# A planner that counts the transfers as one queue, and the loads of a half head as three items

## The chip, the cores and the metric

One core of a Trainium2 chip runs the whole program. The metric is the device time of one execution in microseconds; three runs of the kernel before took 1387.27 to 1389.36, median 1388.89.

## What is computed

One residual block over 1024 tokens of 1024 features, in float32. Cut to what matters here:

```python
h = rms_norm(x, pre_mix_norm)
fq, fk, fv, ff, gq, gk, gv, gb, ga, gz = split(h @ w_in)
# A: 8 heads of 64, causal attention with a bias of gate sums
logits = q @ k.T * scale + cum[q] - cum[k]          # masked
fox_o = rms_norm(softmax(logits) @ v)
# B: 4 heads of 128, delta rule by chunks, then a scan over the chunks
m = strict(k_beta @ k.T * decay);  t_inv = inverse(eye + m)
u = t_inv @ v_beta;  w = t_inv @ (k_beta * exp(gc))
v_new = u - w @ state;  o = q_dec @ state + a_intra @ v_new
state = state * g_last + k_dec.T @ v_new
gdn_o = rms_norm(o) * silu(gz)
x = x + rms_norm(concat(fox_o, gdn_o) @ w_out)
x = x + rms_norm(square(relu(rms_norm(x) @ w_up)) @ w_down)
```

## The kernel before

The program has four stages: the input projection (to about 312 us; its results go to DRAM and come back head by head), the heads' stage (to about 639 us), the output projection, and the two products of the feed-forward part. The change touches the heads' stage alone.

Work of the heads' stage is cut into items. For each of four heads p of kind B there are *fills* (a PSUM bank filled by four transposes or by four or eight products of 128 x 128, then read by one other engine): turned inputs (fv, k, q, v, z), the turned keys knT, the products N (the matrix to be inverted) and A, then X, TX and XR, which build the inverse level by level, and at last W and U. The smallest blocks of the inverse, 16 x 16, are made on DVE: SP's item *gather* brings the diagonal blocks of n_low to DRAM and into 64 lanes (lane_n), DVE's four *lane* items invert them, and SP's *scatter* brings lane_t by way of t_dram into t_low. X and XR at the first level need t_low. I call the time from the last N product to the first X product a lane phase; there are four. The chunks' *scan* (scan_v, scan_o on PE, v_new and state on DVE, o on ACT) follows for each head. Beside that run 64 *tiles* of attention of kind A, eight for each of the eight half heads n: queries (high part on ACT, low part q_lo on POOL), scores (PE), max (DVE, the row minimum), exp (ACT), turn and copy (PE, then ACT or DVE), pv (PE), out (ACT). A half head needs its keys kk_raw (split by ACT and DVE into k_hi and k_lo), its queries q2 (two buffers) and its gate sums cum_row (two buffers). The item *fox* of SP, load_fox, issued all three: kk and q2 as two transfers of 256 KB each, cum as one of 512 KB. Every other load of a head (c_raw_k, q, v, z, v_fox, the decay row) has 512 KB, w_out_raw too. The ends of heads are *tails*: a mean on DVE, a power on POOL, and norms on DVE.

The order is made when the program is built. plan (line 514 on) simulates five queues (PE, ACT, DVE, POOL, SP) with a cost for each item, takes at each step the item that can start first, and breaks ties by the longest way to the end, which is times FOX_SHARE for attention items. follows (and pe_follows to sp_follows) tells what an item waits for. For SP, sp_cost (line 280) gave each item a time held and a time to landing, whatever else was under way. Each engine then runs its items strictly in the order ORDER, so a wait of one item holds all behind it on its engine. On PE, fills take turns in three banks.

At the end of the stage POOL makes eight low parts of w_out (big_lo, w_lo_part), and the first mixed tile is turned on PE (turn_mixed) when the norm that norms_of(0) counts is done, in the order of DVE's norms.

Of the kernel before, what the change touches and what calls it, by code (L numbers as in the profile page):

```python
# [18 lines left out]
NT = SEQ // P  # L19
# [191 lines left out]
for _c in range(KT):  # L211
# [11 lines left out]
    "sp": [(("load", "fv", 0), 0.0), (("load", "k", 0), 0.0), (("load", "v", 0), 0.4), (("load", "fox", 0), 1.7), (("load", "q", 0), 2.9),  # L223
           (("load", "g", 0), 5.2), (("load", "z", 0), 19.9), (("stored",), 22.7), (("load", "fox", 1), 28.2)],
# [55 lines left out]
def sp_cost(item):  # L280

    if item[0] in ("gather", "scatter"):
        return (5.6, 7.0) if item[0] == "gather" else (6.0, 6.9)
    return (3.2, 6.5) if item[:2] == ("load", "fox") else (0.45, 4.5)


def times_of(engine, item):

    if engine == "sp":
        return sp_cost(item)  # L290
    cost = {"pe": pe_cost, "act": act_cost, "dve": dve_cost, "pool": pool_cost}[engine](item)
    return cost - OVERLAP[engine], cost + PASSED_ON[engine]
# [64 lines left out]
def act_follows(kind, n=None, c=0):  # L357
# [14 lines left out]
    if kind == "exp":  # L372
        return [("dve", "max", n)] + [("dve", "tail_mean", ("fox", n // NT - 2, n % NT // HT))] * (n >= 2 * NT and n % HT == 0)
# [22 lines left out]
def dve_follows(kind, n, c=0):  # L396
# [42 lines left out]
def pool_follows(kind, n):  # L439
# [9 lines left out]
    if kind == "z":  # L449
        return [reader((n, "z", 1, 0))]  # L450
# [3 lines left out]
def sp_follows(kind, what, n=0):  # L454
# [8 lines left out]
    if what == "fox":  # L463
        return [("dve", "k_lo", n - 1), ("pool", "queries", NT * (n - 1) - 1), ("dve", "max", NT * (n - 1) - 1)]
# [47 lines left out]
def plan():  # L512
# [7 lines left out]
    free, fills, open_keys = dict(FREE_FROM), [item[1] for item in order["pe"] if item[0] == "fill"], set(keys)  # L520
# [12 lines left out]
    while open_keys:  # L533
# [8 lines left out]
        held, passed = times_of(key[0], key[1:])  # L542
        free[key[0]], done[key] = start + held, start + passed
# [10 lines left out]
FOX_SHARE = 1.0  # L554
# [128 lines left out]
def build(nc, x, pre_mix_norm, w_in, fox_f_bias, fox_out_norm, gdn_conv_w, gdn_a_log,  # L683
# [7 lines left out]
    with ExitStack() as ctx:  # L691
# [593 lines left out]
        def _(sp):  # L1285
# [188 lines left out]
            for item in ORDER["sp"][len(BEGUN["sp"]):]:  # L1474
# [10 lines left out]
                if what == "fox":  # L1485
                    load_fox(n)
# [1553 lines left out]
        def _(pe):  # L3040
# [242 lines left out]
            def scan_second(h, c):  # L3283
# [238 lines left out]
```

## Time and profile before

| | |
|---|---|
| median of 3 runs | 1388.89 us (1387.27 to 1389.36) |
| the profiled execution, device time | 1389.17 us |
| its span | 1386.7 us |
| PE busy in the span | 1319.8 us, 95% |
| DVE, ACT, POOL busy | 918.7, 645.6, 540.9 us |
| mean granted clock of PE | 0.979 |
| DMA, mean over the span | 129 GB/s |

All durations below are of the one profiled execution. Its times count from the start of the span; the device time is 2.5 us longer than the span. A granted clock of 1.00 is 2.4 GHz, one of 0.50 is 1.2 GHz; a value between is a mean over a stretch.

### The profile page before, as it was taken

What the parts mean: (1) busy time and instruction counts of PE and PEld (TensorE: products, weight loads), DVE (VectorE), ACT (ScalarE), POOL (GpSimd) and SP (SyncE); (2) the same over time, 40 slices, a digit from 0 to 9 for tenths busy, and PEclk for the clock granted to TensorE, in tenths of its full rate; (3) what the DMA queues carried; (4) which work ended last, traced back from release to release, by engine and by line L of the source; (5) the groups of instructions that cost most, each with busy time, mean ns of one, the idle gap of its engine ahead of it and who ended that gap; (6) DMA issues with size and microseconds to landing.
All of it is one profiled execution on the core that took longest, in us unless ns stands there. A gap on an engine that the chain in (4) does not pass through costs nothing.

```text
span 1386.7 us, 19443 instructions
## 1 busy us (share of the span) xinstructions
PE 1319.8 (95%) x6800; PEld 1111.0 (80%) x6800; DVE 918.7 (66%) x1506; ACT 645.6 (47%) x1381; POOL 540.9 (39%) x438
## 2 busy tenths in 40 slices
PE   5999999998899999998999899999999999999996
PEld 4778888887798989887887688888887888888885
DVE  6977776657678786753557996555555674444567
ACT  6655333446657576663335332333322444445453
POOL 3742333214423332334013776656563354441001
PEclk9999999999899999998999999999999999999999
DMA  6233223346514142043222455434535983334433
GB/s 198 62 123 121 78 85 112 122 152 204 162 33 123 46 119 57 9 107 92 82 85 77 122 188 167 149 125 143 167 137 192 374 283 99 99 94 159 157 93 150
DMA packets 145319, 178.58 MB, mean 129 GB/s; under 512 B 19852, under 2 KB 92860, under 8 KB 145224
## 3 DMA queue, kind: packets, MB, share of 16 engines
q1 hardware_dynamic: 145224, 177.35, 40.0%
q8 instruction: 55, 0.90, 0.3%
q14 instruction: 40, 0.33, 0.1%
HBM read 124.31 MB, written 53.00 MB: 128 GB/s over the span
## 4 chain that ended last, share of the span: by engine, by line
PE 78%; DVE 11%; DMA 3%; issue 3%; ACT 3%; POOL 1%; SPq 1%; DVEq 0%; ACTq 0%; POOLq 0%
PE ps L3425 7%; PE ps L3427 7%; PE ps L3426 7%; PE ps L3438 6%; PE ps L3439 6%; PE ps L3440 6%; PE ps L3082 6%; PE ps L3084 6%; PE ps L3083 6%; PE ps L3131 5%; PE ps L3266 3%; PE ps L3377 2%; PE ps L3379 2%; PE ps L3378 2%; PE ps L3252 2%
## 5 line engine op out<-in xcount | busy, mean ns | idle before, releaser
L3438 PE MATMUL ps<-db_hi,da_hi 128*128 128x512 f32 x448 | 175.3, 391 | 4.0 <-DVE db_lo L2718 4.0
L3439 PE MATMUL ps<-db_lo,da_hi 128*128 128x512 f32 x448 | 174.4, 389 | 0.0
L3440 PE MATMUL ps<-db_hi,da_lo 128*128 128x512 f32 x448 | 174.3, 389 | 0.0
L2716 DVE TENSOR_TENSOR da_lo<-a_raw,da_hi 128x512 fp32r<-128x512 f32 x112 | 85.6, 764 | 121.0 <-ACT da_hi L2124 120.9
L2124 ACT ACTIVATE da_hi<-a_raw 128x512 fp32r<-128x512 f32 x112 | 70.7, 631 | 159.1 <-PE ps L3440 138.1
L3425 PE MATMUL ps<-bt_hi,ring_hi 128*128 128x512 f32 x320 | 127.2, 397 | 5.1 <-DVE ring_lo L2638 5.1
L3427 PE MATMUL ps<-bt_hi,ring_lo 128*128 128x512 f32 x320 | 126.1, 394 | 0.0
L3426 PE MATMUL ps<-bt_lo,ring_hi 128*128 128x512 f32 x320 | 125.7, 393 | 0.0
L3082 PE MATMUL ps<-i_bt_hi,i_ring_hi 128*128 128x512 f32 x280 | 111.0, 396 | 3.0 <-DVE i_ring_lo L2216 1.6
L3084 PE MATMUL ps<-i_bt_hi,i_ring_lo 128*128 128x512 f32 x280 | 110.3, 394 | 0.0
L3083 PE MATMUL ps<-i_bt_lo,i_ring_hi 128*128 128x512 f32 x280 | 110.0, 393 | 0.0
L3438 PEld LDWEIGHTS ps<-db_hi,da_hi 128*128 128x128 f32 x448 | 84.1, 188 | 24.9 <-DVE db_lo L2718 7.7
L3440 PEld LDWEIGHTS ps<-db_hi,da_lo 128*128 128x128 f32 x448 | 84.1, 188 | 17.7
L3439 PEld LDWEIGHTS ps<-db_lo,da_hi 128*128 128x128 f32 x448 | 84.1, 188 | 17.0
L2948 POOL TENSOR_TENSOR o_rs<-o_ms,halves 128x1 f32<-128x1 f32 x24 | 16.5, 687 | 206.2 <-DVE o_ms L2616 94.7
L2023 ACT ACTIVATE ring_hi<-s_w 128x512 fp32r<-128x512 f32 x64 | 40.3, 632 | 120.6 <-PE ps L3427 118.9
L2718 DVE TENSOR_TENSOR db_lo<-wd,db_hi 128x512 fp32r<-128x512 f32 x112 | 88.7, 792 | 0.0
L2895 POOL TENSOR_TENSOR q_lo<-q,q_hi 128x128 fp32r<-128x128 f32 x64 | 31.1, 486 | 129.9 <-ACT q_hi L1860 127.3
L3266 PE MATMUL ps<-v_tok,probs_t 128*128 128x64 f32 x576 | 80.4, 278 | 1.4 <-ACT probs_t L1849 1.2
L3266 PEld LDWEIGHTS ps<-v_tok,probs_t 128*128 128x128 f32 x576 | 76.6, 202 | 2.8 <-ACT probs_t L1849 2.0
L3425 PEld LDWEIGHTS ps<-bt_hi,ring_hi 128*128 128x128 f32 x320 | 60.8, 190 | 18.5 <-DVE ring_lo L2638 5.6
L3427 PEld LDWEIGHTS ps<-bt_hi,ring_lo 128*128 128x128 f32 x320 | 60.6, 189 | 14.3
(382 smaller groups left out, 3447.7 us busy)
## 6 DMA issues: line engine op xcount, KB each, us to landing
a_raw<-act_dram SPq DMA_DIRECT2D x112, 256.0 KB, 2.6
act_dram<-s_act SPq DMA_DIRECT2D x64, 256.0 KB, 2.2
wd<-in_w_down_dram SPq DMA_DIRECT2D x15, 1024.0 KB, 7.7
act_dram<-c SPq DMA_DIRECT2D x48, 256.0 KB, 4.8
w_top<-in_w_up_dram SPq DMA_DIRECT2D x18, 512.0 KB, 4.2
w_bot<-in_w_up_dram SPq DMA_DIRECT2D x16, 512.0 KB, 5.4
i_top<-in_w_in_dram SPq DMA_DIRECT2D x14, 512.0 KB, 3.9
i_bot<-in_w_in_dram SPq DMA_DIRECT2D x14, 512.0 KB, 5.2
```

The lines of the kernel that those rows point to most:

```text
L2716: nc.vector.tensor_tensor(da_lo[s][:, :], a_raw[n % 4][:, :], da_hi[s][:, :].bitcast(F32), ALU.subtract).then_inc(d_lo_ready, 1)
L2718: nc.vector.tensor_tensor(db_lo[s][:, :], d_moving(n), db_hi[s][:, :].bitcast(F32), ALU.subtract).then_inc(d_lo_ready, 1)
L3082: nc.tensor.matmul(acc, i_ring_hi[r][:, k, :], b_hi[:, k, :], start=(first and k == 0), stop=False, skip_group_check=True)
L3083: nc.tensor.matmul(acc, i_ring_hi[r][:, k, :], b_lo[:, k, :], start=False, stop=False, skip_group_check=True)
L3084: last = nc.tensor.matmul(acc, i_ring_lo[r][:, k, :], b_hi[:, k, :], start=False, stop=(k == HK - 1), skip_group_check=True)
L3266: last = nc.tensor.matmul(fox_o(i)[:, 0:FOX_DIM], probs_t[n % 2][:, kb - 4 * c, :], v_tok[h % 2][:, kb, hh * FOX_DIM:(hh + 1) * FOX_DIM], ...
L3425: nc.tensor.matmul(acc, ring_hi[r][:, k, :], b_hi[:, k, :], start=(first and k == 0), stop=False, skip_group_check=True)
L3426: nc.tensor.matmul(acc, ring_hi[r][:, k, :], b_lo[:, k, :], start=False, stop=False, skip_group_check=True)
L3427: last = nc.tensor.matmul(acc, ring_lo[r][:, k, :], b_hi[:, k, :], start=False, stop=(k == HK - 1), skip_group_check=True)
L3438: nc.tensor.matmul(acc, da_hi[s][:, cols], db_hi[s][:, :], start=start, stop=False, skip_group_check=True)
L3439: nc.tensor.matmul(acc, da_hi[s][:, cols], db_lo[s][:, :], start=False, stop=False, skip_group_check=True)
L3440: return nc.tensor.matmul(acc, da_lo[s][:, cols], db_hi[s][:, :], start=False, stop=stop, skip_group_check=True)
```

## The change

The item ("load", "fox", n) becomes three, ("load", "kk", n), ("load", "q2", n) and ("load", "cum", n), each with its own condition. The planner keeps a time `wire` up to which the transfers are busy: a load lands no sooner than the queue of transfers ahead of it allows, and gather and scatter are made of hops and of eight pieces. Some conditions that the order of an engine must keep are added (exp after exp, o_square after o_square, z after z). FOX_SHARE goes from 1.0 to 0.9. A condition on the banks of the late scan in scan_second now names the first late item of the list. No instruction is added or removed; all five orders are new from the third item or so on.

```diff
-            to("sp", "load", "fox", n)
+            for what in ("kk", "q2", "cum"):
+                to("sp", "load", what, n)
...
-def sp_cost(item):
-
-    if item[0] in ("gather", "scatter"):
-        return (5.6, 7.0) if item[0] == "gather" else (6.0, 6.9)
-    return (3.2, 6.5) if item[:2] == ("load", "fox") else (0.45, 4.5)
+HOP, PIECES, PIECE_LANDS = 1.95, 3.8, 1.6
+
+
+def sp_times(item, start, wire):
+
+    if item[0] == "gather":
+        hop = max(start + PIECES, wire) + PIECE_LANDS
+        return hop + 0.5, hop + 0.1 + HOP, wire
+    if item[0] == "scatter":
+        hop = max(start, wire) + HOP
+        return hop + PIECES, hop + PIECES + PIECE_LANDS, wire
+    count = 2 if item[1] in ("kk", "q2") else 1
+    wire = max(start + 2.3, wire) + (2.2 if item[:2] == ("load", "g") else 1.12 * count)
+    return start + 0.5 * count, wire + 0.2, wire
...
     if kind == "exp":
-        return [("dve", "max", n)] + [("dve", "tail_mean", ("fox", n // NT - 2, n % NT // HT))] * (n >= 2 * NT and n % HT == 0)
+        return [("dve", "max", n)] + [("act", "exp", n - 1)] * (n >= 1) + [("dve", "tail_mean", ("fox", n // NT - 2, n % NT // HT))] * (n >= 2 * NT and n % HT == 0)
...
-    if what == "fox":
-        return [("dve", "k_lo", n - 1), ("pool", "queries", NT * (n - 1) - 1), ("dve", "max", NT * (n - 1) - 1)]
+    if what in ("kk", "q2", "cum"):
+        return [("dve", "k_lo", n - 1) if what == "kk" else ("pool", "queries", NT * (n - 1) - 1) if what == "q2" else ("dve", "max", NT * (n - 1) - 1)]
...
-        held, passed = times_of(key[0], key[1:])
-        free[key[0]], done[key] = start + held, start + passed
+        if key[0] == "sp":
+            free["sp"], done[key], wire = sp_times(key[1:], start, wire)
+        else:
+            held, passed = times_of(key[0], key[1:])
+            free[key[0]], done[key] = start + held, start + passed
...
-FOX_SHARE = 1.0
+FOX_SHARE = 0.9
...
-                if what == "fox":
-                    load_fox(n)
+                if what == "kk":
+                    load_kk(n)
+                elif what == "q2":
+                    load_q2(n)
+                elif what == "cum":
+                    load_cum(n)
...
-                if late and c == 0:
+                if (h, c) == LATE_SCANS[0]:
                     fills_read()
-                elif late:
+                if late and c > 0:
                     pe.wait_ge(o_read, n)
```

**SP in the first lane phase**, from the decay row of head 1, which follows the gather (n_dram, lane_n), to the scatter (t_dram, t_low). q_ is the buffer q2, v_fox the item fv. Before:

```order
L1364 DMA decay<-gate_dram 128x1024 [waits dve_prep]
L1359 DMA v_fox<-proj_dram 128x1024 [waits proj_stored1,filled]
L1353 DMA c_raw_z<-proj_dram 128x1024 [waits proj_stored1,filled]
L1407 DMA w_out_raw_135<-in_w_out_dram 128x8x128
L1374 DMA kk_raw<-proj_dram 64x1024 [waits proj_stored1,k_lo_ready]
L1374 DMA kk_raw<-proj_dram 64x1024
L1383 DMA q_0_145<-proj_dram 64x1024 [waits proj_stored1,q_ready]
L1383 DMA q_0_145<-proj_dram 64x1024
L1393 DMA cum_row_164<-gate_dram 128x1024 [waits fox_max]
L1353 DMA c_raw_z<-proj_dram 128x1024 [waits proj_stored1,filled]
L1462 DMA t_dram<-lane_t 64x256 [waits lane_step]
L1471 DMA t_low<-t_dram 16x8x16 [waits cleared,lanes_moved]
```

And now:

```order
L1380 DMA decay<-gate_dram 128x1024 [waits dve_prep]
L1369 DMA c_raw_q<-proj_dram 128x1024 [waits proj_stored0,pool_prep,filled]
L1399 DMA q_0_145<-proj_dram 64x1024 [waits proj_stored1,q_ready]
L1399 DMA q_0_145<-proj_dram 64x1024
L1375 DMA v_fox<-proj_dram 128x1024 [waits proj_stored1,filled]
L1390 DMA kk_raw<-proj_dram 64x1024 [waits proj_stored1,k_lo_ready]
L1390 DMA kk_raw<-proj_dram 64x1024
L1369 DMA c_raw_z<-proj_dram 128x1024 [waits proj_stored1,filled]
L1423 DMA w_out_raw_135<-in_w_out_dram 128x8x128
L1409 DMA cum_row_164<-gate_dram 128x1024 [waits fox_max]
L1478 DMA t_dram<-lane_t 64x256 [waits lane_step]
L1487 DMA t_low<-t_dram 16x8x16 [waits cleared,lanes_moved]
```

The queries c_raw_q of head 1 stood ahead of the gather and now come behind it; kk of half head 2 has gone ahead of the gather, and kk of half head 3 has come in; the z load of head 2 (the second c_raw_z of before) now follows the scatter. PE's fills of these queries, which stood 17.9 us of work into the stage's list, now stand at 22.7, those of z at 27.1 instead of 23.6.

**POOL at the start of the stage**, from the clearing of t_low. Before:

```order
L2921 MEMSET t_low 128x1024 [waits i_done,i_lo_ready]
L2895 TENSOR_TENSOR q_lo_172<-q_0_145,q_hi_170 128x128 [waits q_hi_ready]
L2864 TENSOR_TENSOR powers<-means,plus_half 128x4 [waits dve_prep] x2
L2879 TENSOR_TENSOR kd_147<-kn,gates_all 128x512 [waits filled,dve_prep]
L2869 TENSOR_TENSOR decay<-decay,const 128x1024 [waits act_prep]
```

And now:

```order
L2941 MEMSET t_low 128x1024 [waits i_done,i_lo_ready]
L2884 TENSOR_TENSOR powers<-means,plus_half 128x4 [waits dve_prep]
L2915 TENSOR_TENSOR q_lo_172<-q_0_145,q_hi_170 128x128 [waits q_hi_ready]
L2884 TENSOR_TENSOR powers<-means,plus_half 128x4 [waits dve_prep]
L2899 TENSOR_TENSOR kd_147<-kn,gates_all 128x512 [waits filled,dve_prep]
```

One power has gone ahead of the first low half of the queries.

**DVE at the end of the stage**, to the first low part of the turned mixed tiles (fox_rr and fox_ms are the mean of half head 7's second half, gdn_ms those of head 3, mixed_half the norms). Before:

```order
L2509 SCALAR_TENSOR_TENSOR fox_rr<-row_sum 128x4 [waits fox_read]
L2511 TENSOR_TENSOR fox_ms<-fox_ss,fox_rr 128x4 [waits rr_ready]
L2495 SCALAR_TENSOR_TENSOR state<-state,g_last_179,ps 128x128 [waits state_ready,scan_done]
L2505 TENSOR_TENSOR gdn_ms<-gdn_ss,q_eps 128x4 [waits gdn_square_done]
L2519 SCALAR_TENSOR_TENSOR mixed_half_160<-mixed_half_160,fox_ms,fox_norm_row 128x64 [waits masks_ready,tail_power] x4
L2527 SCALAR_TENSOR_TENSOR mixed_half_159<-mixed_half_159,gdn_ms,z_tok_158 128x128 [waits z_normed,tail_power] x4
L2527 SCALAR_TENSOR_TENSOR mixed_half_160<-mixed_half_160,gdn_ms,z_tok_158 128x128 [waits z_normed,tail_power] x4
```

And now:

```order
L2525 TENSOR_TENSOR gdn_ms<-gdn_ss,q_eps 128x4 [waits gdn_square_done]
L2529 SCALAR_TENSOR_TENSOR fox_rr<-row_sum 128x4 [waits fox_read]
L2531 TENSOR_TENSOR fox_ms<-fox_ss,fox_rr 128x4 [waits rr_ready]
L2547 SCALAR_TENSOR_TENSOR mixed_half_159<-mixed_half_159,gdn_ms,z_tok_158 128x128 [waits z_normed,tail_power] x4
L2547 SCALAR_TENSOR_TENSOR mixed_half_160<-mixed_half_160,gdn_ms,z_tok_158 128x128 [waits z_normed,tail_power] x4
L2539 SCALAR_TENSOR_TENSOR mixed_half_160<-mixed_half_160,fox_ms,fox_norm_row 128x64 [waits masks_ready,tail_power] x4
```

The norms of head 3 now stand ahead of those of half head 7's second half; POOL's last three powers have changed places in the same way, and among its eight big_lo parts POOL has one more low half of queries and one power.

## Rows read from the trace of the kernel before

**Rows 1.** Stretches: length, busy (x) of PE, PEld, DVE, ACT, POOL, PEclk, DMA share, GB/s.
```profile
350.00:380.00 30.00, 24.44 (x152) 21.90 (x150) 20.41 (x54) 19.07 (x61) 13.58 (x12) 0.77 0.59 165
380.00:420.00 40.00, 39.84 (x345) 38.19 (x345) 29.94 (x81) 22.28 (x74) 9.99 (x13) 1.00 0.16 43
420.00:445.00 25.00, 22.18 (x154) 20.29 (x152) 20.26 (x56) 17.73 (x60) 8.52 (x8) 0.86 0.55 156
...
490.00:510.00 20.00, 16.80 (x115) 14.65 (x115) 17.81 (x47) 16.28 (x57) 10.13 (x11) 0.91 0.32 90
...
570.00:593.00 23.00, 19.64 (x136) 18.11 (x136) 15.83 (x52) 12.07 (x43) 6.56 (x8) 0.85 0.07 12
...
632.00:650.00 18.00, 13.19 (x62) 11.32 (x62) 8.32 (x21) 3.83 (x11) 7.31 (x6) 0.72 0.40 118
```

**Rows 2.** Waits of PE, 320 to 640 us: us in total, times, longest.
```profile
PE ps L3234 <- DVE row_min L2477: 5.1, 7, 1.2
PE ps L3355 <- DVE mixed_half L2527: 4.0, 1, 4.0
```

**Rows 3.** Timeline, start of the stage: start us, us, engine, line, instruction [idle <-releaser].
```profile
323.96 0.83 POOL L2895 TENSOR_TENSOR q_lo<-q,q_hi 128x128 fp32r<-128x128 f32 x1
...
326.18 0.66 PE L3136 MATMUL ps<-const,kn 128*128 128x128 f32 x4 [0.83 <-DVE kbg L2375]
```

**Rows 4.** Chain of waits at full clock: start us, us, what (x matmuls).
```profile
590.93 0.89 PE ps L3266 x8
...
597.27 0.89 PE ps L3131 x8
...
602.74 0.87 PE ps L3136 x8
```

**Rows 5.** First lane phase: SP's timeline, landings, chain, PE's timeline.
```profile
343.88 0.32 SPq L1353 DMA_DIRECT2D c_raw_q<-proj_dram  x1
344.29 3.71 SPq L1454 DMA_DIRECT2D n_dram<-n_low  x8
...
351.60 0.58 SPq L1364 DMA_DIRECT2D decay<-gate_dram  x1
...
368.62 3.63 SPq L1471 DMA_DIRECT2D t_low<-t_dram  x8
...
DMA to landing us min/median/max: 1.5/1.7/2.2
...
352.76 6.20 DMA c_raw_z<-proj_dram
...
359.10 1.09 PE L3136 MATMUL ps<-const,c_raw_z 128*128 128x128 f32 x4 [2.61 <-DMA c_raw_z<-proj_dram]
...
375.06 1.11 PE L3131 MATMUL ps<-t_low,n_low 128*128 128x128 f32 x8
```

**Rows 6.** Fourth lane phase: timeline of DVE, then of PE.
```profile
580.48 1.39 DVE L2424 TENSOR_TENSOR lane_p<-lane_t,lane_x 64x512 f32<-64x512 f32 x1
581.91 0.68 DVE L2427 TENSOR_REDUCE lane_t<-lane_p 64x64 f32<-64x512 f32 x1
...
583.29 0.77 PE L3281 MATMUL ps<-state,w_all 128*128 128x128 f32 x2 [2.11 <-ACT mixed_half L1895]
```

**Rows 7.** The hand-over: timelines of POOL, DVE and PE, then one group of the page.
```profile
617.60 18.65 POOL L2910 TENSOR_TENSOR big_lo<-w_out_raw,big_hi 128x1024 fp32r<-128x1024 f32 x8 [1.71 <-ACT big_hi L1914]
636.54 1.01 POOL L2903 TENSOR_TENSOR fox_ms<-fox_ms,minus_half 128x4 f32<-128x4 f32 x1 [0.29 <-DVE fox_ms L2511]
...
634.77 1.50 DVE L2509 SCALAR_TENSOR_TENSOR fox_rr<-row_sum 128x4 f32<-128x4 f32 x1 [1.01 <-ACT sq_fox L1884]
...
638.56 2.19 DVE L2527 SCALAR_TENSOR_TENSOR mixed_half<-mixed_half,gdn_ms,z_tok 128x128 f32<-128x128 f32 x8
...
639.01 2.37 PE L3355 MATMUL ps<-const,mixed_half 128*128 128x128 f32 x10 [4.01 <-DVE mixed_half L2527]
...
L2895 POOL TENSOR_TENSOR q_lo<-q,q_hi 128x128 fp32r<-128x128 f32 x64 | 31.1, 486 | 129.9 <-ACT q_hi L1860 127.3
```

More of the change, by code:

```diff
@@ L222 @@
     "pool": [],
-    "sp": [(("load", "fv", 0), 0.0), (("load", "k", 0), 0.0), (("load", "v", 0), 0.4), (("load", "fox", 0), 1.7), (("load", "q", 0), 2.9),
-           (("load", "g", 0), 5.2), (("load", "z", 0), 19.9), (("stored",), 22.7), (("load", "fox", 1), 28.2)],
+    "sp": [(("load", "fv", 0), 0.0), (("load", "k", 0), 0.0), (("load", "v", 0), 0.4), (("load", "kk", 0), 0.0),
+           (("load", "q2", 0), 0.0), (("load", "cum", 0), 1.7), (("load", "q", 0), 2.9), (("load", "g", 0), 5.2), (("load", "z", 0), 20.6),
+           (("stored",), 23.4), (("load", "kk", 1), 25.6), (("load", "q2", 1), 27.8), (("load", "cum", 1), 29.0)],
 }
@@ L277, in pool_cost @@
     return {"power": 1.02, "decay": 2.37, "kd": 1.05, "qd": 2.37, "queries": 0.47, "z": 2.4, "tail_power": 1.02, "w_out": 2.37}[item[0]]
-def sp_cost(item):
-    if item[0] in ("gather", "scatter"):
-        return (5.6, 7.0) if item[0] == "gather" else (6.0, 6.9)
-    return (3.2, 6.5) if item[:2] == ("load", "fox") else (0.45, 4.5)
+HOP, PIECES, PIECE_LANDS = 1.95, 3.8, 1.6
[9 more added lines that the diff above has]
+    return start + 0.5 * count, wire + 0.2, wire
 def times_of(engine, item):
     if engine == "sp":
-        return sp_cost(item)
+        held, lands, _ = sp_times(item, 0.0, 0.0)
+        return held, lands
     cost = {"pe": pe_cost, "act": act_cost, "dve": dve_cost, "pool": pool_cost}[engine](item)
@@ L380, in act_follows @@
     if kind == "o_square":
-        return [("act", "o", n, c)] + [("dve", "tail_mean", ("gdn", n - 1, c // HT))] * (n >= 1 and c % HT == 0)
+        before = divmod(NCHUNK * n + c - 1, NCHUNK)
+        return [("act", "o", n, c)] + [("act", "o_square") + before] * (n + c >= 1) + [("dve", "tail_mean", ("gdn", n - 1, c // HT))] * (n >= 1 and c % HT == 0)
     if kind == "queries":
-        return [("sp", "load", "fox", n // NT)] + [("pe", "scores", n - 2)] * (n >= 2) + [("act", "queries", n - 1)] * (n >= 1)
+        return [("sp", "load", "q2", n // NT)] + [("pe", "scores", n - 2)] * (n >= 2) + [("act", "queries", n - 1)] * (n >= 1)
     if kind == "k_hi":
-        return [("sp", "load", "fox", n)] + [("act", "out", 0)] * (n == 1) + [("pe", "scores", NT * (n - 1) - 1)] * (n >= 3)
+        return [("sp", "load", "kk", n)] + [("act", "out", 0)] * (n == 1) + [("pe", "scores", NT * (n - 1) - 1)] * (n >= 3)
     last = GDN_HEADS - 1
@@ L422, in dve_follows @@
         before = FOX_TILES[n - 2][2] // 4
-        return [("pe", "scores", n)] + [("sp", "load", "fox", n // NT)] * (n % NT == 0) + [("pe", "turn", n - 2, before)] * (n >= 2)
+        return [("pe", "scores", n)] + [("sp", "load", "cum", n // NT)] * (n % NT == 0) + [("pe", "turn", n - 2, before)] * (n >= 2)
     if kind == "k_lo":
@@ L479, in is_fox @@
 def is_fox(item):
-    return item[0] in FOX_KINDS or item[:2] in (("load", "fox"), ("tail_norm", "fox")) or (item[0] in ("tail_mean", "tail_power") and item[1][0] == "fox")
+    return item[0] in FOX_KINDS or item[:2] in (("load", "kk"), ("load", "q2"), ("load", "cum"), ("tail_norm", "fox")) or (item[0] in ("tail_mean", "tail_power") and item[1][0] == "fox")
 def ways_to_end(before):
@@ L519, in plan @@
     early = {key: before[key] + bank_follows(key, before) for key in keys}
-    free, fills, open_keys = dict(FREE_FROM), [item[1] for item in order["pe"] if item[0] == "fill"], set(keys)
+    wire, free, fills, open_keys = 0.0, dict(FREE_FROM), [item[1] for item in order["pe"] if item[0] == "fill"], set(keys)
     waiting, ready = {}, {engine: {} for engine in ENGINES}
```

2 lines of the change are left out of this document (1 added, 1 removed).

## The prediction

> **What bounds the kernel now.** I read the page first, then the table of stretches, the waits of PE, the queue of SP, and last the two stalls and the hand-over one instruction at a time. PE is busy for 95% of the span, so only a stretch in which it is not can give or lose much. The heads' stage runs from about 312 to 639 us. Between its four lane phases PE is full: 39.84 of 40.00 us at the full clock [rows 1]. Around each lane phase it is not: 24.44 of 30 us at a granted clock of 0.77, 22.18 of 25 at 0.86, 16.80 of 20 at 0.91, 19.64 of 23 at 0.85. Idle time there is 5.6 + 2.8 + 3.2 + 3.4 = 15.0 us. The missing clock (2.4 GHz falls to 1.2 behind each gap) costs about 0.23 x 30 + 0.14 x 25 + 0.09 x 20 + 0.15 x 23 = 15.7 us more, if all of it is PE-bound. The hand-over to the output projection has 4.8 us idle and a clock of 0.72.
>
> The causes are small and many: scores that wait for DVE's row minimum 5.1 us in 7 waits, one 4.0 us wait at the hand-over [rows 2], 2.61 us for one load, z [rows 5]. No wait of PE is put down to the keys, queries or gate sums of a half head. So the new split of "fox" into three items removes no wait by itself. What counts is the other order that the planner writes on all five queues.
>
> **The change, part by part.** The same instructions run: 469 items on PE before and after. Hence every term is idle time or clock, not work.
>
> *Start.* POOL now makes a power ahead of the first low half of the queries. Before, that low half ran 323.96 to 324.79 and PE waited for it; a power takes 1.01 [rows 7]. PE's next item waits until 326.18 anyway for DVE [rows 3]. The scores' chain goes 1.0 us later, of which the latter wait hides most: **+0.4** (ends 0 and +1.0).
>
> *First lane phase.* Between the last N product and the first X product PE has, by its order, 19.7 us of work before and 24.1 after. (I added the items at their length at full clock: four transposes 0.44, eight products 0.89, a block of probabilities times values 0.21, from [rows 4]; score products come on top.) Before, the gather was issued at 344.29, t_low landed 1.7 us after the last of the issues that begin at 368.62 and take 3.63, so at 374.0, and X began at 375.06 [rows 5]. So 31 us passed over 19.7 us of work. More cover would be worth 4.4 us if the 31 us stood. But two loads that PE needs inside move back on SP's queue. The queries of head 1 (c_raw_q) were issued at 343.88, before the gather; now they come behind it and behind the decay row, at about 352.2. The z load was issued at 352.76 and PE waited 2.61 us for it; now the queries, two q2 halves and two kk halves stand ahead of it too. From 351.6 to 358.96 decay row, v_fox and z, 1.5 MB, came in; less the 1.7 us that even a small transfer takes to land that is 280 GB/s, or 1.9 us each. With six such loads behind the gather instead of three, queries land at about 357.5 and z at 364.5. PE reaches the queries 11.2 us of work after N, near 355, and z 4.4 us of work later: waits of about 2.5 and 2 us. The time then is 24.1 + 4.5 + 1.1 of smaller waits + 3.4 to 6.8 for the clock, 33 to 36 us, against 31 + 4.4 before: **-1.0** (ends -4.4, both loads in time, and +3, both late and one low stretch more). t_dram also loses a z load with a wait of its own ahead of it; as many megabytes as before stand there, so I count nothing.
>
> By the Trainium skill, "DMA: Bandwidth & Descriptors", section on the anatomy of one DMA, a transfer costs about 2.0 us plus its bytes over 436 GB/s: six loads would be in after 9.2 us, z at about 361, and this term would be near -3. The rows have the three loads of before in after 7.4 us, where it gives 5.6, so I keep mine.
>
> *Second and third.* Work between N and X falls from 20.0 to 18.3 and from 19.8 to 18.7 us. Were the wait for t_low the bound, this would cost 1.7 and 1.1. It isn't quite: PE's gaps there are DVE's (row minimum, 5.1 us), whose queue holds the lane work, in the fourth phase to 582.59 [rows 6]. In the third, DVE has one row minimum fewer inside the lane work, but SP carries five loads between gather and scatter (cum, kk, v, q, z) that were after it or ahead. **0 each** (ends -1 and +1.7; -1.5 and +2.5).
>
> *Fourth.* Cover grows from 19.1 to 21.5 us, SP carries nothing between. But PE's 2.11 us gap was set by DVE: the state update that PE's product needs came behind two lane operations that begin at 580.48, and PE got it at 583.29. Such a chain stays. **-1.0** (ends 0; -5.8 if the gap is gone with its low stretch, 2.4 + 3.4).
>
> *Hand-over.* PE ends its scan at about 635.0 and starts the transposes at 639.01. Between lie POOL's eight big_lo parts until 636.25, DVE's fox_rr that took 1.50 us beside them, a power 1.01, and a second power, that of gdn, before the first norm at 638.56 [rows 7]. Tile 0 needs that norm of gdn, and not of fox 7's second half. In the new order both gdn powers and norms stand before those. POOL's eight parts can start 2.8 us of PE work earlier against PE's end (the last W fill has 18.7 us of work behind it instead of 15.9) and get a low half (0.49) and a power (1.01) between them: end at about 634.9. Then power 635.9, norm 0.36, PE at 636.5: **-2.5** (ends -2.8 and, if POOL ends no earlier, +0.5).
>
> The skill's "SBUF — State Buffer", section on who interferes with whom, says that a DVE instruction with two SBUF inputs blocks against a GpSimd one that reads SBUF, for its whole length. By it the norm could wait for the second power and the term be -1.5; in the row eight norms ran in 2.19 us beside such a power, so I keep -2.5.
>
> The sum is 0.4 - 1.0 + 0 + 0 - 1.0 - 2.5 = **-4.1 us**. On the profiled execution, 1389.17 us, that is 1385.1; the median of the runs is 0.3 lower, so I say **1384.8 us**. About 0.2% (2.8 us) is what a measurement of this kernel can tell from no change.
>
> **The rivals.**
>
> A, *slower: the loads behind the first gather.* If six loads take their full turn and PE waits 3 us for the queries and 3 for z, the clock falls twice, and the thinner cover of the second and third phases costs its 2.8. Then +3 + 2.8 + 0.4 - 1 - 2.5 = +2.7, and with one more low stretch of 6.8 us (3.4) +6: 1391.5 to 1395. For it: the DMA share is 0.59 over that stretch and PE did wait for z. Against: its z item stands 3.5 us of work later. It decides once z lands more than 6 us after PE gets to the queries. 22%.
>
> B, *the plan is right.* The cover holds in the first and fourth phase, and a low stretch goes with one of them: -4.4 - 2.4 - 3.4 - 2.5 + 0.4 = -12.3, 1376.6. For it: gaps and clock there are 30 us. Against: most gaps are DVE's, and DVE's work is the same. 15%.
>
> C, *nothing moves.* The hand-over gives 2.5 and the phases take it back, or POOL ends no earlier: 1388. The loads were never waited for, so the split does not do what its name says. 20%.
>
> **How the numbers follow.** My forecast, 1381 to 1386, has 43%. Faster by over 0.2%: 43 + 15 = 58%; within: 20%; slower: 22%. The range leaves out the far half of B and of A's upper end: 1378 to 1392.
>
> **What the profile after would show.** First transposes of mixed tiles about 2.5 us sooner after the last scan product, with a gdn norm as releaser. In the first phase a wait of PE for c_raw_q or c_raw_z of 2 us or so. In the fourth a gap below 2 us. Quiet stretches still full. I am wrong if PE's idle time in the four phases changes by more than 4 us in sum, if a new wait for a kk, q2 or cum load appears, or if the hand-over still takes 4 us.

## The result, and the profile after

The changed kernel takes 1405.41 us (median of 4 runs, 1403.59 to 1410.78), the kernel before 1389.12 beside it (1387.27 to 1390.62): ratio 1.0116, 95% interval 1.0082 to 1.0150. It is 16.3 us slower. I had said 1384.8 and a range to 1392. The profiled execution took 1410.78, the slowest of the four and 5.4 above their median; its span is 1408.3. So its rows show somewhat more loss than the median has. Line numbers after the change are 20 higher on the compute engines and 16 higher on SP.

The stretches of [rows 1], and three at the end of the stage, in the same columns:

```profile
350.00:380.00 30.00, 24.65 (x157) 21.88 (x157) 19.98 (x61) 20.54 (x70) 13.31 (x13) 0.83 0.65 166
380.00:420.00 40.00, 39.44 (x342) 37.85 (x341) 30.05 (x76) 20.46 (x63) 8.73 (x12) 1.00 0.18 57
420.00:445.00 25.00, 17.57 (x113) 15.55 (x112) 19.48 (x49) 16.12 (x55) 9.16 (x9) 0.80 0.43 110
...
490.00:510.00 20.00, 15.92 (x114) 14.14 (x112) 17.83 (x47) 10.30 (x40) 7.64 (x7) 0.83 0.62 170
...
570.00:593.00 23.00, 19.88 (x146) 18.24 (x146) 20.09 (x64) 13.40 (x52) 8.04 (x9) 0.90 0.08 12
...
632.00:640.00 8.00, 4.10 (x31) 3.37 (x29) 7.88 (x10) 7.60 (x18) 7.71 (x5) 0.99 0.10 29
640.00:660.00 20.00, 14.68 (x87) 13.90 (x88) 10.15 (x23) 6.90 (x26) 11.09 (x7) 0.66 0.18 59
660.00:680.00 20.00, 18.03 (x74) 14.79 (x73) 4.58 (x12) 3.05 (x4) 0.41 (x2) 0.74 0.34 99
```

The first phase (350 to 380) is as good as before. The second (420 to 445) has 7.4 us idle instead of 2.8. The worst lies where I had forecast the best gain, from 632 on. PE's waits (us in total, times, longest), 310 to 665 us, against [rows 2]:

```profile
PE ps L3301 <- DVE state L2515: 6.9, 1, 6.9
PE ps L3272 <- DVE probs_t L2487: 6.7, 5, 3.1
PE ps L3156 <- DMA c_raw_q<-proj_dram: 6.1, 2, 3.2
PE ps L3254 <- DVE row_min L2497: 4.3, 6, 1.2
```

Three are new: one wait of 6.9 us for a state of the scan, one of 3.1 for turned probabilities, and two for the queries. Here is the first, in the timelines of DVE, POOL and PE:

```profile
633.19 0.16 DVE L2531 TENSOR_TENSOR fox_ms<-fox_ss,fox_rr 128x4 f32<-128x4 f32 x1
...
634.78 8.99 DVE L2539 SCALAR_TENSOR_TENSOR mixed_half<-mixed_half,fox_ms,fox_norm_row 128x64 f32<-128x64 f32 x4
643.70 0.34 DVE L2515 SCALAR_TENSOR_TENSOR state<-state,g_last,ps 128x128 f32<-128x128 f32 x1
...
634.40 11.60 POOL L2930 TENSOR_TENSOR big_lo<-w_out_raw,big_hi 128x1024 fp32r<-128x1024 f32 x5
...
644.09 0.80 PE L3301 MATMUL ps<-state,w_all 128*128 128x128 f32 x2 [6.91 <-DVE state L2515]
```

Four norms of fox 7 take 8.99 us. Each takes 0.2 to 0.3 elsewhere. They lie beside five big_lo parts of POOL at 2.3 us each. Taken one by one, the parts end at 636.79, 639.10, 641.40 and 643.70, and the four norms at 636.87, 639.18, 641.48 and 643.78: each norm is over 0.08 us behind the end of a part, and then the next part has begun. One norm gets in at each seam. The state update queued behind them on DVE is late, and PE's scan with it. In the kernel before the same four norms stood ahead of big_lo. No row calls this a wait of DVE: the time stands in the *duration* of the norms. The second new wait has the same shape (DVE, then POOL):

```profile
437.41 2.22 DVE L2529 SCALAR_TENSOR_TENSOR fox_rr<-row_sum 128x4 f32<-128x4 f32 x1
439.66 2.27 DVE L2531 TENSOR_TENSOR fox_ms<-fox_ss,fox_rr 128x4 f32<-128x4 f32 x1
...
437.26 2.35 POOL L2889 TENSOR_TENSOR decay<-decay,const 128x1024 f32<-128x1024 f32 x1 [1.76 <-ACT qdT L1817]
439.56 2.36 POOL L2905 TENSOR_TENSOR qdT<-qdT,c_raw_q 128x1024 f32<-128x1024 f32 x1
```

To place the loss, I take the time from one gather's first issue to the next and from the last to the first mixed transposes, and subtract PE's work between them as each order has it, at the lengths of [rows 4]. What is left, against the kernel before:

| us | start | gather 0 to 1 | 1 to 2 | 2 to 3 | 3 to transposes | sum |
|---|---|---|---|---|---|---|
| forecast | +0.4 | -1.0 | 0 | 0 | -1.0 - 2.5 | -4.1 |
| after | +0.8 | +0.3 | +4.9 | +3.4 | +11.1 | +20.5 |
| run e1 | +2.4 | -0.3 | +2.9 | +3.1 | -1.3 | +6.8 |
| run e6 | +2.1 | -1.5 | -0.6 | +2.7 | -1.4 | +1.3 |

These are single records: e8 below, in which nothing ahead of the hand-over is changed, differs from the kernel before by 2.3 us in one of these columns. So only large entries say anything.

### The profile page after: what moved, and what is told of

Read it like the earlier page. It is cut to its first block, busy times and chain, and to the rows that moved or that the text cites. A ratio compares the mean times of both kernels' runs of the same rounds, so it can differ in the third digit from the quotient of the medians.

```text
span 1408.3 us, 19444 instructions
## 1 busy us (share of the span) xinstructions
PE 1330.0 (94%) x6800; PEld 1120.8 (80%) x6800; DVE 926.4 (66%) x1506; ACT 646.7 (46%) x1381; POOL 540.9 (38%) x438
## 4 chain that ended last, share of the span: by engine, by line
PE 80%; DVE 11%; ACT 3%; DMA 2%; issue 2%; SPq 1%; POOL 1%; DVEq 0%; ACTq 0%; POOLq 0%
PE ps L3445 7%; PE ps L3447 7%; PE ps L3446 7%; PE ps L3458 6%; PE ps L3460 6%; PE ps L3459 6%; PE ps L3102 6%; PE ps L3104 5%; PE ps L3103 5%; PE ps L3151 5%; PE ps L3286 4%; PE ps L3397 2%; PE ps L3399 2%; PE ps L3398 2%; PE ps L3156 2%
## 5 line engine op out<-in xcount | busy, mean ns | idle before, releaser
L3286 PE MATMUL ps<-v_tok,probs_t 128*128 128x64 f32 x576 | 84.5, 289 | 1.6 <-ACT w_all L1861 0.6
L3286 PEld LDWEIGHTS ps<-v_tok,probs_t 128*128 128x128 f32 x576 | 81.1, 213 | 3.1 <-issue 2.4
```

What stands on the lines that cost most here:

```text
L3286: last = nc.tensor.matmul(fox_o(i)[:, 0:FOX_DIM], probs_t[n % 2][:, kb - 4 * c, :], v_tok[h % 2][:, kb, hh * FOX_DIM:(hh + 1) * FOX_DIM], ...
```

## The experiments

The runs were made to decide between two theories. T1: a DVE instruction that needs the SBUF port that POOL reads by waits out POOL's running instruction, and what stands behind it on DVE's queue is late for PE. T2: the loads behind the gather and the thinner cover in the lane phases cost the time. Medians that follow are beside medians of the kernel before on the same chip, 1389.3 to 1390.0 us.

### e1, e2: the four norms alone, away and back

```diff
+moved("dve", [("tail_norm", "fox", (7, k)) for k in range(4)], ("tail_norm", "gdn", (3, 0)))   # e1, on the changed kernel
+moved("dve", [("tail_norm", "fox", (7, k)) for k in range(4)], ("state", 3, 4))                # e2, on the kernel before
```

(moved takes items out of an engine's order and puts them ahead of the item named last.)

> The changed kernel, with the four norms of fox 7's first half tile moved on DVE's queue to behind the last state update (just ahead of the first norm of gdn 3). Theory T1 (a DVE instruction with two SBUF inputs cannot run while POOL is in an instruction that reads SBUF, and here holds back the state update that the last scan products wait for): the four norms took 8.99 us beside POOL's big_lo parts against 0.2 to 0.3 each elsewhere, and PE waited 6.91 us for the state behind them. Off the queue's path, that wait goes, the clock behind it stays up, and the kernel is 6 to 9 us faster than the changed one: about 1397.5 where the changed one has 1405.4, ratio to the kernel before 1.006. Theory T2 (the loads behind the first gather and the thinner cover in the lane phases cost the time): less than 2 us changes, 1404 to 1406, ratio 1.011.

> The kernel before, with the same four norms moved the other way: from ahead of POOL's big_lo parts to beside them, ahead of the state update of chunk 4 of head 3. Nothing else of the change is in it. T1: the norms stretch to about 2.3 us each, one for each big_lo part, PE gets its state 6 to 7 us late, and the kernel is 6 to 9 us slower: 1395 to 1398, ratio 1.005. T2: four norms of 0.2 to 0.3 us in another place, no change beyond 1 us, 1388 to 1390, ratio 1.000.

e1: 1391.81 us, ratio 1.0020 (1.0004 to 1.0037). e2: 1398.59, ratio 1.0074 (1.0050 to 1.0099). In e2 (DVE, then PE):

```profile
625.23 7.96 DVE L2529 SCALAR_TENSOR_TENSOR mixed_half<-mixed_half,fox_ms,fox_norm_row 128x64 f32<-128x64 f32 x4
...
633.51 0.80 PE L3291 MATMUL ps<-state,w_all 128*128 128x128 f32 x2 [7.03 <-DVE state L2505]
```

T1 holds in both directions: moving four short instructions gives back 13.6 of the 16.3 us, and putting them beside big_lo in the kernel before costs 9.0. The size in e1 is above my 6 to 9. The wait is 6.9; that leaves 6.7, which I put down to the clock. The profiles fit that, though no run changes the clock by itself. In the changed kernel the granted clock is 0.66 from 640 to 660 and 0.74 from 660 to 680, 12 us of missing clock: PE stood still from 637 to 644, and from 644 to 653 the granted clock was 0.50, that is 1.2 GHz; it was 0.50 again from 662 to 668, behind the waits of 1.23 and 1.97 us at the hand-over. In e1 the same two stretches are

```profile
640.00:660.00 20.00, 16.34 (x86) 14.00 (x86) 9.48 (x24) 4.38 (x16) 7.10 (x6) 0.91 0.34 106
660.00:680.00 20.00, 20.00 (x101) 16.76 (x100) 8.44 (x10) 6.12 (x9) 1.64 (x3) 1.00 0.15 53
```

or 1.8 us missing (the kernel before has 0.80 and 1.00 there, 4.0 us). e2 paid less, 9.0 us for a wait of 7.0. Its stretches of 632 to 640, 640 to 660 and 660 to 680 have 0.50, 0.82 and 1.00, against 0.86, 0.80 and 1.00 in the kernel before: 2.5 us more missing.

### e14: what in the instruction makes it wait

```diff
+                if n == 7 and qb < HT:
+                    nc.vector.tensor_scalar(o, o, fox_ms[:, n % 2, qb:qb + 1], None, ALU.mult).then_inc(mixed_ready, 1)
+                    return
```

> The changed kernel with fox 7's first four norms where the change put them, beside big_lo, but as instructions with one SBUF input (o times a scalar, without the product with fox_norm_row, which these four tiles leave out). If it is the second SBUF input that makes a DVE instruction wait out POOL's, they take 0.2 us each, the wait of 6.91 us goes, and the kernel is at e1's 1392, ratio 1.002. If any DVE instruction that may use both read ports is held (q_eps, with one input, took 1.50 and 2.10 us beside decay and z against 0.17 alone), they take 2.3 us each as before and the kernel stays at 1403 to 1406, ratio 1.011.

This kernel leaves out the product of these four tiles with fox_norm_row; it serves the timing alone. 1405.71 us, ratio 1.0110 (1.0081 to 1.0139), on a level with the changed kernel. DVE, then PE:

```profile
628.67 8.96 DVE L2540 TENSOR_SCALAR mixed_half<-mixed_half,fox_ms 128x64 f32<-128x64 f32 x4
...
637.93 0.79 PE L3304 MATMUL ps<-state,w_all 128*128 128x128 f32 x2 [6.87 <-DVE state L2515]
```

It isn't the second input. One SBUF input in this form waits just as long. What passes freely beside big_lo, in e1's timelines of DVE and POOL: v_new at 0.29 and state at 0.35 us, which read PSUM and one SBUF tensor (state a column of scalars from SBUF besides), and the copies of probabilities from PSUM.

```profile
638.23 0.35 DVE L2525 SCALAR_TENSOR_TENSOR state<-state,g_last,ps 128x128 f32<-128x128 f32 x1 [0.56 <-PE ps L3338]
640.41 0.29 DVE L2514 TENSOR_TENSOR v_new<-u_all,ps 128x128 f32<-128x128 f32 x1 [1.83 <-PE ps L3311]
...
629.95 13.99 POOL L2940 TENSOR_TENSOR big_lo<-w_out_raw,big_hi 128x1024 fp32r<-128x1024 f32 x6
```

Beside decay a TENSOR_REDUCE from SBUF took its usual 0.69, and the TENSOR_SCALAR behind it 1.50 against 0.17 alone (e6, DVE, then POOL):

```profile
434.69 0.69 DVE L2385 TENSOR_REDUCE q_sums<-q_sq 128x4 f32<-128x512 f32 x1
435.41 1.50 DVE L2387 TENSOR_SCALAR q_eps<-q_sums 128x4 f32<-128x4 f32 x1
...
434.53 2.34 POOL L2901 TENSOR_TENSOR decay<-decay,const 128x1024 f32<-128x1024 f32 x1 [1.48 <-ACT qdT L1829]
```

The Trainium skill, "SBUF — State Buffer", § who interferes with whom, says this: two SBUF inputs contend with a GpSimd instruction that reads SBUF, tensor_scalar and copy contend when they enter a mode that takes both ports, tensor_reduce never does, and the one that starts first holds the port for its whole length. The runs agree beside POOL's instructions over 128x1024; no run has a copy out of SBUF there. Beside POOL's powers, over 128x4, the rows of the kernel before don't show the lock (DVE, then POOL):

```profile
637.58 0.87 DVE L2519 SCALAR_TENSOR_TENSOR mixed_half<-mixed_half,fox_ms,fox_norm_row 128x64 f32<-128x64 f32 x4 [0.78 <-POOL fox_ms L2903]
...
637.52 1.98 POOL L2905 TENSOR_TENSOR gdn_ms<-gdn_ms,minus_half 128x4 f32<-128x4 f32 x2
```

Four norms with two SBUF inputs ran there in 0.87 us, all within the first of two powers of 1.01 us. Why they pass is open. The wait can fall on POOL too: in e4 its qdT took 3.34 us when DVE's k_split, held by decay until 436.63, still ran until 437.72, against 2.36.

### e5, e6: the loads, and the second phase

```diff
+moved("sp", [("load", "q", 1)], ("gather", 0))                          # e5, on e1
+moved("sp", [("load", "q", 2)], ("load", "g", 2))
+moved("dve", [("tail_mean", ("fox", 2, 0))], ("tail_mean", ("gdn", 0, 1)))   # e6, on e1
+moved("dve", [("tail_norm", "fox", (2, 0))], ("tail_norm", "fox", (2, 1)))
```

> On top of the first experiment's edit (norms of fox 7 behind the last state, 1391.8 us, ratio 1.002): on SP's queue the load of head 1's queries goes ahead of the first gather, and that of head 2's ahead of the decay row of head 2. T2 (the loads behind the gather cost time of their own): the waits of PE for c_raw_q, 2.4 to 3.2 us in the first phase and up to 2.8 in the second, go, and the kernel is 2 to 5 us faster than the first experiment, 1387 to 1390. T1 (only port waits count, the load waits are cover for the later lane phase's end, because the next limit, t_low or DVE, comes as late as before): the waits go, X starts no sooner, within 1 us: 1391 to 1393.

> On top of the first experiment's edit: on DVE's queue the mean of fox 2's first half (fox_rr and fox_ms, two instructions that took 2.21 and 2.27 us beside POOL's decay and qdT, against 0.15 and 0.16 alone) and the norm behind it go past two copies of probabilities and two row minima. T1: PE's wait of 3.06 to 3.57 us for probs_t near 442 falls below 1 us, and the kernel is 2 to 5 us faster than the first experiment, 1387 to 1390. T2: POOL's decay and qdT have nothing to do with it, another DVE or DMA wait takes its place: within 1 us of 1391.8.

e5: 1392.37 us, ratio 1.0027 (1.0017 to 1.0038). The waits for c_raw_q are gone, and X comes 31.7 us behind the gather instead of 34.2, but the time is e1's. The wait that the loads cost is real in the record, and what its end gave was lost again by the end of the fourth phase (clock 0.78 there against 0.89 in e1). So the part of T2 that is about the loads of the queries accounts for none of the 16 us, as far as this run can tell. The thinner cover was not tested by itself.

e6: 1389.95 us, ratio 1.0003 (0.9991 to 1.0015), about 2 us faster than e1, though the two intervals overlap. DVE, then PE:

```profile
438.30 0.92 DVE L2541 SCALAR_TENSOR_TENSOR fox_rr<-row_sum 128x4 f32<-128x4 f32 x1
439.26 0.16 DVE L2543 TENSOR_TENSOR fox_ms<-fox_ss,fox_rr 128x4 f32<-128x4 f32 x1
...
435.15 0.44 PE L3284 MATMUL ps<-const,probs 128*128 128x128 f32 x2 [1.29 <-ACT probs_t L1881]
```

The wait of 3.57 us that e1 had there is gone. With e1's and e6's moves, six DVE items in all, the changed kernel is level with the kernel before. It keeps the change's loads and cover, so these cost little. It also keeps the new order at the hand-over; e8 below has that order with the old lane phases and is 3.4 us faster by the medians (the intervals overlap a little). About so much the new order may still cost in the lane phases.

### e3, e4, e11: which part of the change writes such an order

```diff
-FOX_SHARE = 1.0
+FOX_SHARE = 0.9      # e3, on the kernel before; e4 is the reverse, on the changed kernel
```

> The kernel before with the planner's share of fox work at 0.9 and none of the rest of the change. Its order puts all norms of fox 7's first half behind the last state, and two row maxima between lane operations in the first phase. T1: no norm stands beside big_lo, so the hand-over does not lose its 7 us; what it does to the phases is open: 1386 to 1393. T2, as far as it is a matter of the share (cover between N and X 20.9, 18.6, 20.2 and 18.4 us of PE's work against 19.7, 20.0, 19.8 and 19.1 before): 1389 to 1392. If the share alone made the loss of 16 us, this kernel is near 1405.

> The changed kernel with the share of fox work back at 1.0, so the new costs of the transfers and the three items of a load alone. Its order has the norms of fox 7 ahead of big_lo, as before, and 21.7, 17.6, 22.0 and 18.5 us of PE's work between N and X in the four phases. T1: the 6.9 us wait at the hand-over is gone and the kernel is at least 6 us faster than the changed one, 1392 to 1399. T2: the loads behind the first gather stay and the cover is thinner in the second and fourth phase than in the changed kernel: 1404 to 1408.

e3: 1391.85 us, ratio 1.0026 (1.0010 to 1.0042). e4: 1402.30, ratio 1.0104 (1.0075 to 1.0133), where I expected the wait's end to make it at least 6 us faster than the changed kernel. The norms are ahead of big_lo in e4, yet two other things went wrong. DVE, then POOL:

```profile
434.46 3.25 DVE L2362 TENSOR_TENSOR k_split<-kk_raw,k_split 64x1024 fp32r<-64x1024 f32 x1
...
506.22 2.27 DVE L2531 TENSOR_TENSOR fox_ms<-fox_ss,fox_rr 128x4 f32<-128x4 f32 x1
...
631.97 18.57 POOL L2930 TENSOR_TENSOR big_lo<-w_out_raw,big_hi 128x1024 fp32r<-128x1024 f32 x8 [15.91 <-ACT big_hi L1934]
```

Other DVE items stand beside POOL's large ones (1.22 and 0.16 us alone). And POOL's 18.6 us of big_lo begin when the last W fill is read; e4's order has 12.0 us of PE's work behind that fill, the kernel before 15.9, the changed one 18.7. e11 moves five DVE items of e4 away:

```diff
+moved("dve", [("k_lo", 4)], ("read", (1, "X", 0, 4)))
+moved("dve", [("tail_mean", ("fox", 3, 1)), ("tail_mean", ("fox", 4, 0))], ("tail_norm", "gdn", (1, 4)))
+moved("dve", [("tail_mean", ("gdn", 3, 0)), ("tail_mean", ("fox", 7, 1))], ("tail_mean", ("gdn", 3, 1)))
```

> The changed kernel with the share at 1.0 (the fourth run, 1402.3 us, ratio 1.010), and five DVE items moved out from beside POOL's large instructions: the low half of head 4's keys (3.25 us beside decay, 1.22 alone) past two row minima, the means of fox 3's second and fox 4's first half (2.27 us beside z) past two row minima, the means of gdn 3's first and fox 7's second half (1.58 and 0.81 + 2.26 us beside big_lo) behind the last state. T1: the waits of 2.00 (probs_t), 3.40 (row_min) and 2.74 us (v_new) go, with the low clock behind two of them: 5 to 10 us faster than the fourth run, 1392 to 1397. If that run was slow by its order of the lane phases: within 2 us of 1402.

1401.68 us, ratio 1.0086 (1.0068 to 1.0105): 0.6 us better than e4 by the medians, 2.5 by the ratios, which is not clear of noise. A miss. The waits of 2.00, 3.40 and 2.74 us went as expected, and the time came back in one place:

```profile
651.97 3.65 PE L3387 MATMUL ps<-const,mixed_half 128*128 128x128 f32 x16 [6.97 <-DVE mixed_half L2559]
```

In e11 PE ended its scan at 645.0 and POOL its eighth part at 649.2. I read this as two causes of e4's loss, the port and the short cover behind the last W fill: when the first is taken away, the second stands alone. No run has the cover repaired, so the second is argued. By itself the split with the new costs (e4) loses 12.7 us and the share (e3) 2 to 4. The two don't add up to the change's 16: four norms beside big_lo and ahead of a state stand in neither order, only in that of both together.

### p1: a planner that knows the port

```diff
+PORT_DVE = ("lane", "k_lo", "tail_mean", "tail_norm")
...
+            starts = [(max(free[engine], t, bank if key[1] == "fill" else 0.0, port if on_port(key) else 0.0), -way[key], str(key), key)
...
+        if on_port(key):
+            port = free[key[0]]
```

> The changed kernel with a planner that never lets a POOL instruction and DVE's lane work, low halves of keys, means or norms overlap in its plan. T1: fewer of those DVE instructions take 2 us or more than in the changed kernel (mean of lane_p of 512 elements near 1.07 us rather than 1.76), and with 27 us of PE's work between N and X in the first phase it beats the changed kernel by 8 to 20 us: 1385 to 1397. T2: the loads and the cover decide, and it is within 4 us of the changed kernel or slower, 1401 or more. The plan runs ahead of the chip or behind it by a few us, so that the exclusion may miss.

1404.87 us, ratio 1.0116 (1.0096 to 1.0136): no gain. Its norms of fox average 320 ns, against 436 in the changed kernel, but lane_p over 512 elements is still at 1.65 us. Its order has 10.8 us of work behind the last W fill, POOL's big_lo ran from 635.67 to 654.2, and PE, busy for 45.00 of 45 us between 445 and 490 in the changed kernel, was busy for 41.4. Knowing one resource more didn't mend this plan, and no run says which of these made its loss.

### e8, e9, e10, e12, e13, e15: the hand-over

e8 is the kernel before with the change's order at the hand-over and nothing else of it:

```diff
+moved("dve", [("tail_mean", ("gdn", 3, 1)), ("tail_mean", ("fox", 7, 1))] + [("tail_norm", "gdn", (3, k)) for k in range(8)], ("tail_norm", "fox", (7, 4)))
+moved("pool", [("tail_power", ("gdn", 3, 0)), ("tail_power", ("gdn", 3, 1))], ("tail_power", ("fox", 7, 1)))
```

> The kernel before, with the changed kernel's order at the hand-over alone: on POOL both powers of gdn 3 ahead of fox 7's second one, on DVE the mean and the norms of gdn 3 ahead of the mean and norms of fox 7's second half. No port wait is made by it. By the prediction's last term the first transposes come one power (1.0 us) and some of DVE's work sooner behind POOL's last big_lo part: 1 to 2.5 us faster than before, 1387 to 1388.5, ratio 0.998 to 0.999. If the hand-over is bound by POOL's big_lo parts alone, nothing changes: 1389.5.

1386.54 us, ratio 0.9982 (0.9968 to 0.9997), 2.5 us faster than before, or 0.4 to 4.4 by the interval. The term of the prediction that I had for this, -2.5, is met in number. Its working is not: it had POOL's parts end 1.35 us sooner against PE, which e8's order doesn't bring. In the record the transposes waited 2.70 us instead of 4.01, ACT's next step came 0.8 us sooner (below), and the clock from 640 to 660 was 0.95 instead of 0.80, up to 3 us. e9 adds one move on SP:

```diff
+moved("sp", [("scatter", 0)], ("load", "z", 2))
```

> The kernel before, with the hand-over order of the third batch's run e8 (gdn first, ratio 0.998) and one more item moved, on SP's queue: scatter 0 goes ahead of the load of head 2's z. In e8 that load waited until 363.18 for PE to read the buffer it overwrites, and the scatter behind it, whose lanes DVE had ready at 361.3, was issued at 363.55; PE later waited 2.51 us for t_low. If t_low bounds the first lane phase, the wait goes: 1 to 2.5 us faster than e8, near 1384.5. If other waits of that phase take its place (DVE's row minimum, the z load), no change: 1386.5.

1387.31 us, ratio 0.9985 (0.9971 to 1.0000): nothing. The wait for t_low in e8 was one record's. e10 (on e9) and e12 (on e6) put the last big_lo part behind the powers; e12 also moves the mean of gdn 3's first half behind the last state:

```diff
+moved("pool", [("tail_power", ("gdn", 3, 0)), ("tail_power", ("gdn", 3, 1)), ("tail_power", ("fox", 7, 1))], ("w_out", 7))
```

> On top of e9_scatter_first: on POOL the last of the eight big_lo parts goes behind the three powers of the hand-over. If POOL's parts bound the hand-over, the first norm of gdn 3 and the first transposes come 1.0 to 1.5 us sooner; T1 adds that norms which then run beside the late part take up to 2.3 us each, which only fox 7's second half meets: 1382.5 to 1384 where e9 has 1384.5. If PE then waits longer for the mixed tiles' low halves or for big_lo 7, nothing is gained.

> The changed kernel with every move that the runs so far bear out: norms of fox 7 behind the last state, the mean of fox 2 later, the mean of gdn 3's first half (1.95 us beside big_lo) behind the last state too, and the last big_lo part behind the powers. T1: 1 to 2 us faster than e6 (1389.95): 1388 to 1389, on a level with the kernel before. What it still loses against e9 and e10, which have the same hand-over, is then the price of the change's order in the lane phases: 2 to 5 us.

e10: 1387.91 us, ratio 0.9999 (0.9984 to 1.0014). e12: 1392.46, ratio 1.0020 (1.0007 to 1.0034), 2.5 worse than e6. Both miss what I expected. In e10:

```profile
637.70 3.68 PE L3368 MATMUL ps<-const,mixed_half 128*128 128x128 f32 x16 [5.36 <-POOL big_lo L2923]
```

PE has one wait for all eight parts, and it stands ahead of the transposes, which don't read big_lo (line 3342 before the change). I had overlooked it. e15 moves that wait behind the transposes on e8, e13 moves it and the last part:

```diff
-            pe.wait_ge(w_out_lo, KT)
...
                 pe.wait_ge(m_lo_ready, t + 1)
+                if t == 0:
+                    pe.wait_ge(w_out_lo, KT)
```

> The run e8 (gdn first, ratio 0.998) with the last big_lo part behind the three powers, as in e10, and PE's one wait for all eight parts moved from ahead of the first transposes to ahead of the first product that reads big_lo. e10 and e12 lost 5.36 and 4.42 us in that wait. If the powers behind big_lo bound the norms, the first transposes come about 1 us sooner than in e8, and the part is in before the products, which begin 5 us later: 1385 to 1386 where e8 has 1386.5, ratio 0.997. If big_lo's last part is then waited for at the products, or the norms of the second tile are held beside it, 1386.5 to 1389.

> The run e8 with PE's wait for the eight big_lo parts moved alone, POOL's order as in e8. In e8 the first transposes wait for the first norm of gdn 3, which comes 1.3 us behind the last part, so the wait had already passed: no change, ratio 0.998.

e13: 1389.55 us, ratio 1.0001 (0.9988 to 1.0015). e15: 1387.44, ratio 0.9979 (0.9967 to 0.9991), as e8. In e13 (PE, DVE, POOL, ACT):

```profile
638.40 1.97 PE L3366 MATMUL ps<-const,mixed_half 128*128 128x128 f32 x16 [1.32 <-DVE mixed_half L2539]
...
640.10 2.94 DVE L2531 SCALAR_TENSOR_TENSOR mixed_half<-mixed_half,fox_ms,fox_norm_row 128x64 f32<-128x64 f32 x4
...
639.97 2.41 POOL L2922 TENSOR_TENSOR big_lo<-w_out_raw,big_hi 128x1024 fp32r<-128x1024 f32 x1
...
643.08 1.94 ACT L1994 ACTIVATE m_hi<-ps 128x1024 fp32r<-128x1024 f32 x2 [5.48 <-DVE mixed_half L2531]
```

The transposes do come 1.3 us sooner behind the scan than in e15, but ACT's m_hi, the next step, waits for DVE's *last* norm, and the last four norms now take 2.94 us beside the late part instead of 0.86. In the kernel before m_hi began at 641.05, when the first tile's transposes were done, 0.3 us behind the last norm; from e8 on the last norm binds. That wait is the kernel's own: heads_over (line 1036 before the change) holds ACT until every norm is done. From the end of PE's last scan product to m_hi it is 6.05 us before, 5.25 in e8, 5.24 in e15 and 6.00 in e13. e8 and e15 are the versions that beat both kernels.

## Why the prediction was wrong

**Start**, +0.4: right, within what one record can tell (e1 and e6 have +2.4 and +2.1 with the same order there). PE waited 2.94 us for the low half instead of 1.92, and the gather was issued 0.1 us later.

**First lane phase**, -1.0: right in its sum, with one of its waits. The queries were waited for, 3.24 us against my 2.5; z was not. From gather to X 34.0 us passed over 24.1 us of work, in my 33 to 36. That the sum came out is in part luck. The queries landed at 359.59 and z at 367.30, 2.1 and 2.8 us later than I had worked out, and the scatter's first hop, for which I counted nothing, took 8.8 us to land behind these loads instead of 5.0 (t_dram was issued at 362.25 and in at 371.06; before, at 363.60 and 368.61). The section of the Trainium skill on the anatomy of one DMA, by which I had set a number beside this term, is about transfers that GpSimd issues; these are SP's.

**Second**, 0, ends -1 and +1.7: wrong, +4.9. I looked at PE's cover and SP's loads. The change put the mean of fox 2 beside decay and qdT, and e6 takes that back (-0.6, where e1 had +2.9).

**Third**, 0: +3.4, and +2.7 still in e6. In the record a lane operation (2.36 us, at 494.54) lies beside z_tok. No run moved it, so this cause is only argued. The same goes for the **fourth**, where a lane operation took 2.49 us beside z_tok, against 1.07 in the second and third phase.

**Hand-over**, -2.5: met in number by e8, which has the same order alone, and hidden in the changed kernel under the wait for the state. That the changed kernel's transposes waited 1.23 us instead of 4.01 proves nothing, since PE came to them 7 us late; e1, without that wait, has 2.30. I explained the term by the first norm of gdn. That was the bound only until it moved; e8 and e13 show the last norm as the next one.

**The step that failed** is the one sentence in which I set the port aside: "in the row eight norms ran in 2.19 us beside such a power, so I keep -2.5". That row [rows 7] is of a power over 128x4, and I misread it: the power ended at 639.50, so the first three of the eight norms ran within it, the fourth began in it, and the rest ran beside nothing. It was also asked about the wrong instructions: in the changed kernel the norms of gdn 3 took 2.19 us again. The row that mattered stood in the same group: fox_rr, 1.50 us beside big_lo, for an instruction of 128x4. I had used it as a duration, and never asked what else of DVE's the new order puts beside POOL's instructions of 2.3 us. The order of DVE shows it: tail_norm fox 7 0 to 3 ahead of state 3 4, with the last six parts of w_out open on POOL. With the wait priced at what the runs measured, four parts, 9 us less the slack of 2, and 6 us of clock, the sum would have been some 9 us on the slow side. Of my signs of being wrong one was met: PE's idle time in the four phases grew by 5.0 us in sum, from 14.9 to 20.0. None named a DVE instruction that gets longer. Rival A, the slower case, had the wrong mechanism: the waits for queries that e5 takes away gave nothing back in time.

**Rival B's** premise, that the plan is right, falls by p1 and e4 too: both are plans by the same rules, and both lose 12 us and more. Its sum needed the cover in the first and fourth phase to be worth its full length, which no column of the table shows.

## What to carry to other kernels

When instructions change places, list for each engine pair that shares a resource what now runs beside what. A short DVE instruction with its operands in SBUF, placed beside a train of long GpSimd ones, costs up to one GpSimd instruction each (1.1 to 2.4 us here), and what is queued behind it comes late by as much: keep those items off the critical queue's path. Instructions that read PSUM and one SBUF tensor were not held. Look for this in the mean duration of one form, since no row of waits shows it. A gap of 7 us on a full TensorE cost 9 us in one kernel and 13.6 in another, with a low clock behind it: price the gap with the low stretch.

## What the hardware showed that I had not expected

- In a train of GpSimd instructions one DVE instruction gets in at each seam: four norms over four seams, 8.99, 7.96 and 8.96 us in three kernels.
- Smallness doesn't help: instructions of 128x4 took 2.22, 2.27 and, as TENSOR_SCALAR, 1.50 us (e6, 435.41, beside decay), against 0.15 to 0.17.
- But an instruction of POOL over 128x4 held nobody up: four norms ran in 0.87 us within a power of 1.01 us.
- Behind a wait the clock can cost about as much again: 13.6 us came back for a wait of 6.9, and the granted clock was 0.50 for the 9 us behind it.
